# Attention's value products with queries in the partitions, head norms one tick earlier, K's decay copied ahead of the sigmoid, and three reorderings

## The reference, cut to what matters

```python
f = lb + (1.0 - lb) * sigmoid(f_pre);  log_f = log(f);  k = 1.0 - f
# per chunk: b = cumsum(log_f)
# o = (q * exp(b)) @ state + intra-chunk attention
k_dec = kc * exp(b_last - b)
new_state = exp(b_last) * state + k_dec.T @ vc
o = rms_norm(o, hgrn_norm_w) * silu(g_h)     # norm over each head's 128 columns
y = concat([pool_out, o]) @ w_out
```

```python
s = (q_nope @ k_nope.T + q_rope @ k_rope.T) * SCALE      # 8 heads, 512 queries, 768 keys
p = softmax(s);  attn = p @ v                            # v has 64 columns a head
x_mid = layer_norm(ALPHA * x + g1 * (concat([conv, attn]) @ w_o + b_o))
x = layer_norm(ALPHA * x_mid + g2 * (conv_ffn(x_mid * (1 + sc2) + sh2)))
```

## Time and profile before

| what | value |
|---|---|
| median of 3 runs | 1263.81 us (1262.99 to 1265.47) |
| profiled execution, own time | 1265.41 us |
| its span | 1263.6 us |
| TensorE matmuls busy | 1148.3 us (91%) |
| TensorE weight loads busy | 933.3 us (74%) |
| VectorE busy | 847.6 us (67%) |
| ScalarE busy | 561.5 us (44%) |
| GpSimd busy | 163.1 us (13%) |
| mean granted clock of TensorE | 0.971 |
| chain that ended last | TensorE 63%, VectorE 17%, ScalarE 12% |

### The profile page before, as it was taken

One profiled execution on the slowest core, in us unless ns is written; L12 is line 12 of the kernel. 1 busy time (PEld: TensorE's weight loads), 2 busy tenths in 40 slices (PEclk: granted clock), 3 DMA queues, 4 the chain that ended last, 5 costly groups with the idle time before them and its releaser, 6 DMA issues.

```text
span 1263.6 us, 14090 instructions
## 1 busy us (share of the span) xinstructions
PE 1148.3 (91%) x5488; PEld 933.3 (74%) x5488; DVE 847.6 (67%) x1352; ACT 561.5 (44%) x861; POOL 163.1 (13%) x179
## 2 busy tenths in 40 slices
PE   1878989898889998998999998879999999999996
PEld 1657877787778877887887765558888888888885
DVE  5866787877775775455688888838676566665246
ACT  3265445454452332657444565534644444442121
POOL 0033323441444220000000001000000000000000
PEclk9889999999999998998999999989999999999998
DMA  7723132223242567592221010011232222225201
GB/s 283 299 101 134 67 133 101 100 97 137 84 142 91 217 229 201 179 73 70 79 74 42 3 67 34 33 34 67 79 122 100 100 96 84 91 96 183 100 34 66
DMA packets 28306, 136.59 MB, mean 108 GB/s; under 512 B 7760, under 2 KB 8016, under 8 KB 14416
## 3 DMA queue, kind: packets, MB, share of 16 engines
q1 hardware_dynamic: 20448, 128.46, 29.3%
q10 hardware_dynamic: 7792, 7.24, 3.0%
HBM read 133.57 MB, written 2.12 MB: 107 GB/s over the span
## 4 chain that ended last, share of the span: by engine, by line
PE 63%; DVE 17%; ACT 12%; issue 3%; POOL 3%; DMA 2%; DVEq 0%; SPq 0%; ACTq 0%
PE PB L184 62%; ACT L199 4%; DVE RAW L1342 3%; DVE CV L213 3%; ACT WH L198 3%; DVE WL L205 2%; DMA RAW<-in_wstream 1%; DVE PTA L205 1%; DVE UPA L205 1%; POOL UPA L205 1%; DVE PX L236 1%; DMA XL<-in_xT 1%; ACT PTA L199 1%; DVE XL L213 1%; DVE AT L233 1%
## 5 line engine op out<-in xcount | busy, mean ns | idle before, releaser
L184 PE MATMUL PB<-HH,WH 128*128 128x512 f32 (+1 forms) x896 | 354.6, 396 | 18.2 <-DVE WL L205 7.4
L184 PE MATMUL PB<-HL,WH 128*128 128x512 f32 (+1 forms) x896 | 343.1, 383 | 0.0
L184 PE MATMUL PB<-HH,WL 128*128 128x512 f32 (+1 forms) x896 | 343.0, 383 | 0.0
L205 DVE TENSOR_TENSOR WL<-RAW,WH 128x1024 fp32r<-128x1024 f32 (+2 forms) x174 | 201.8, 1166 | 207.5 <-ACT WH L198 206.8
L198 ACT ACTIVATE WH<-RAW 128x1024 fp32r<-128x1024 f32 (+2 forms) x174 | 169.5, 980 | 363.7 <-PE PB L184 328.2
L184 PEld LDWEIGHTS PB<-HH,WH 128*128 128x128 f32 x896 | 172.0, 192 | 52.5 <-DVE WL L205 9.0
L184 PEld LDWEIGHTS PB<-HH,WL 128*128 128x128 f32 x896 | 171.2, 191 | 33.4
L184 PEld LDWEIGHTS PB<-HL,WH 128*128 128x128 f32 x896 | 171.8, 192 | 29.1 <-issue 0.5
L213 DVE SCALAR_TENSOR_TENSOR CV<-VP,PC,CV 128x512 f32<-128x512 f32 x120 | 89.0, 776 | 0.7
L199 ACT ACT_TABLE_LOAD x53 | 68.0, 1283 | 5.5 <-DMA PC<-in_params 4.6
L184 PE MATMUL PB<-WL,AH 128*128 128x512 f32 x176 | 68.5, 389 | 0.0
(11 more groups left out here) (266 smaller groups left out, 1840.8 us busy)
## 6 DMA issues: line engine op xcount, KB each, us to landing
RAW<-in_wstream SPq DMA_DIRECT2D x108, 1024.0 KB, 4.8
RAW<-in_wstream SPq DMA_DIRECT2D x5, 768.0 KB, 4.1
RAW<-in_wstream SPq DMA_DIRECT2D x5, 512.0 KB, 3.4
XL<-in_xT SPq DMA_DIRECT2D x2, 1024.0 KB, 8.5
HB<-in_x SPq DMA_DIRECT2D x2, 1024.0 KB, 6.2
out<-XL SPq DMA_DIRECT2D x8, 256.0 KB, 2.0
ROWS<-in_rows ACTq DMA_DIRECT2D x3, 512.0 KB, 7.6
XC<-in_ctx SPq DMA_DIRECT2D x1, 1024.0 KB, 8.2
```

The costliest lines, as they stand in the source:

```text
L184: return self.put(lambda e: e.matmul(o, l, r, start=start, stop=stop, skip_group_check=skip))
L205: return self.put(lambda e: e.tensor_tensor(o, a, b, op))
```

## The change

The diff does six things.

1. `stream_layout`: for the last pool group (g = 0) the third `also()` is left out; that "a" item and those behind it come one place later in the list.
2. HGRN: the copy into KDT becomes `key_decay` and stands at the head of `head(h, 1)` of the next head, ahead of its sigmoid and logarithm (for head 7 in `pool_gate`); DG, its spread and the product with it come three steps earlier each.
3. Before the second input product, ScalarE and VectorE split fewer blocks ahead of the first tiles of h2, tile 1 follows tile 0, and `y_squares(2, 1)` moves behind a split.
4. Attention: the exponentials become the stationary operand, 128 queries at a time, and V with one column of ones (65 columns) the moving one: four products in place of one, with queries in the partitions. VectorE's `values_out` takes a reciprocal of the sums and multiplies into OT; TensorE's `pair_turn` transposes OT of a pair into a bank of the turn (t = 3 of heads 2, 4 and 6, and at the end), from where ScalarE and VectorE split it. ScalarE's copies, logarithm and exponential and VectorE's pair product go.
5. `conv_square` of tiles that end late comes behind the last exponential.
6. Merge: the first split of the second half comes ahead of the others, and TensorE makes the first block's products of row tiles 3 and 0 of the second half ahead of the rest of the first half.

```diff
@@ -70,7 +70,8 @@
         w(u[1])
-        also()
+        if g:
+            also()
     def rows(name, *tiles):
@@ -470,7 +471,8 @@
     VG = sb("VG", [128, 6, 768], F32, c2)
-    SU = TMP[:, 0:512]
+    OTT = OT[:, :].rearrange("p (j n) -> p j n", n=128)
+    RSUM = TMP[:, 0:4].rearrange("p (j n) -> p j n", n=1)
     CKH, CKL = (z[:, 3:6, :].rearrange("p a n -> p (a n)").rearrange("p (k n) -> p k n", n=NKEY) for z in (CH, CL))
@@ -789,11 +791,6 @@
                 a.act(x, x, ACTF.Exp).then_inc(S_.a_s, ("kd", h))
-            elif step == 8:
-                a.wait_ge(S_.p_sm, ("kt", h))
-                if h:
-                    a.wait_ge(S_.p_sm, ("kv", h - 1))
-                a.copy(KDT[:, :], aux.of(("kt", h))).then_inc(S_.a_ax, ("kt", h))
             elif step == 13:
@@ -806,9 +803,17 @@
                     hgrn(h, step)
+        def key_decay(h):
+            a.wait_ge(S_.p_sm, ("kt", h))
+            if h:
+                a.wait_ge(S_.p_sm, ("kv", h - 1))
+            a.copy(KDT[:, :], aux.of(("kt", h))).then_inc(S_.a_ax, ("kt", h))
         def head(h, b):
...
             z = main.of(("z", h, b))
+            if h and b == 1:
+                key_decay(h - 1)
             a.wait_ge(S_.p_blk, 4 * h + b)
@@ -893,6 +898,8 @@
             after(nb)
+            if p == 3 and m:
+                key_decay(7)
             if p == 3:
@@ -1045,14 +1052,15 @@
         shifted(1)
-        y_squares(2, 1)
         split(B_IN2)
-        split(B_IN2 + 1)
         split(B_IN2 + 2)
         h_tile("h2", 0, 0, M2, SC1)
+        h_tile("h2", 1, 0, M2, SC1)
+        split(B_IN2 + 3)
+        y_squares(2, 1)
         y_squares(3, 1)
-        split(B_IN2 + 3)
-        for k in range(1, 8):
+        split(B_IN2 + 1)
+        for k in range(2, 8):
             h_tile("h2", k, 0, M2, SC1)
@@ -1163,26 +1171,9 @@
             a.act(PR[s % 3], main.of(("s", h, t)), ACTF.Exp, scale=SCALE).then_inc(S_.a_ev, ("s", h, t))
-        def values_out(h):
-            me, other = ((0, 64), (64, 128)) if h % 2 == 0 else ((64, 128), (0, 64))
-            z = aux.of(("ov", h))
-            a.wait_ge(S_.p_sm, ("o", h, 5))
-            if h > 1:
-                a.wait_ge(S_.v_h, ("m", 4 + h // 2 - 1))
-            a.copy(OT[me[0]:me[1], :], z[me[0]:me[1], :])
-            a.copy(SU[me[0]:me[1], :], z[other[0]:other[1], :]).then_inc(S_.a_ax, ("ov", h))
-        def pair_divisor(p):
-            a.wait_ge(S_.a_ax, ("ov", 2 * p + 1))
-            a.act(SU, SU, ACTF.Ln).then_inc(S_.a_s)
-            a.wait_ge(S_.a_s)
-            a.act(SU, SU, ACTF.Exp, scale=-1.0).then_inc(S_.a_s, ("su", p))
         def pair_high(p):
-            a.wait_ge(S_.v_s, ("pair", p))
-            a.copy(MH[:, 4 + p, :], OT[:, :]).then_inc(S_.a_h, ("m", 4 + p))
+            a.wait_ge(S_.p_sm, ("ot", p))
+            a.copy(MH[:, 4 + p, :], main.of(("ot", p))).then_inc(S_.a_h, ("m", 4 + p))
         def conv_square(j):
@@ -1215,10 +1206,6 @@
                     split(KEY_BLOCK[(h + 1) // 2] + NW)
-                if t == 1 and h:
-                    values_out(h - 1)
-                if t == 2 and h % 2 == 0 and h:
-                    pair_divisor(h // 2 - 1)
                 if 1 <= t <= 4 and h < 7:
@@ -1234,18 +1221,17 @@
                 for j in range(4):
-                    if CONV_END[j] != "end" and 6 * CONV_END[j][0] + CONV_END[j][1] + 2 == 6 * h + t:
+                    if CONV_END[j] != "end" and 6 * CONV_END[j][0] + CONV_END[j][1] + 2 == 6 * h + t < 44:
                         conv_square(j)
...
             a.dma(row, VEC[1 + n:2 + n, :].partition_broadcast(128)).then_inc(S_.row, *["o"] * n, by=16)
-        values_out(7)
         for j in range(4):
-            if CONV_END[j] == "end" or 6 * CONV_END[j][0] + CONV_END[j][1] + 2 >= 48:
+            if CONV_END[j] == "end" or 6 * CONV_END[j][0] + CONV_END[j][1] + 2 >= 44:
                 conv_square(j)
-        pair_divisor(3)
         pair_high(3)
+        split(B_O + NW)
         for j in range(4):
@@ -1264,7 +1250,7 @@
                 .then_inc(S_.a_st, (stage, "q", i, h))
-        for nb in range(B_O, B_O + 4):
+        for nb in range(B_O + 1, B_O + 4):
             split(nb + NW)
@@ -1470,11 +1456,11 @@
                     .then_inc(S_.v_ax, ("st", h))
-            elif step == 18:
+            elif step == 15:
                 v.wait_ge(S_.g_s, ("pow", h))
...
                 diag(DG, sct(h % 2)[:, 4:8], 4, ("dg", h))
-            elif step == 21:
+            elif step == 18:
                 v.wait_ge(S_.p_sm, ("dg", h))
@@ -1658,13 +1644,14 @@
         x1(1)
-        for n in range(3):
-            split(B_IN2 + n)
         gated(3, 1)
+        split(B_IN2)
+        split(B_IN2 + 2)
         h_low("h2", 0, 0)
+        h_low("h2", 1, 0)
+        split(B_IN2 + 3)
         before_power(1)
-        split(B_IN2 + 3)
-        h_low("h2", 1, 0)
+        split(B_IN2 + 1)
         before_second(1)
@@ -1797,13 +1784,24 @@
             v.maxneg(NM[:, c:c + 1], PB[2 + (j % 2 if h == 0 else 0)][:, 0:NKEY]).then_inc(S_.v_ax, ("mx", h, j), ("mx2", h, j))
-        def pair(p):
-            v.wait_ge(S_.a_s, ("su", p))
-            v.tt(OT[:, :], OT[:, :], SU, MUL).then_inc(S_.v_s, ("pair", p))
+        def values_out(h):
+            z = aux.of(("ov", h))[:, 0:260].rearrange("p (j n) -> p j n", n=65)
+            o, one = (1, 0) if h % 2 else (0, 64)
+            v.wait_ge(S_.p_sm, ("o", h, 5))
+            if h > 1:
+                v.wait_ge(S_.p_sm, ("ot", h // 2 - 1))
+            if h:
+                v.wait_ge(S_.v_ax, ("ov", h - 1))
+            v.recip(RSUM[:, :, :], z[:, :, one:one + 1]).then_inc(S_.v_s)
+            v.wait_ge(S_.v_s)
+            v.tt(OTT[:, :, 64 * (h % 2):64 * (h % 2) + 64], z[:, :, o:o + 64], RSUM[:, :, :].broadcast_to([128, 4, 64]), MUL)\
+                .then_inc(S_.v_ax, ("ov", h))
         def pair_low(p):
-            lo(ML[:, 4 + p, :], OT[:, :], MH[:, 4 + p, :], ("m", 4 + p), ("m", 4 + p))
+            v.wait_ge(S_.a_h, ("m", 4 + p))
+            v.tt(ML[:, 4 + p, :], main.of(("ot", p)), MH[:, 4 + p, :].bitcast(F32), SUB).then_inc(S_.v_ev, ("ot", p))
         query(0)
@@ -1821,6 +1819,8 @@
             for t in range(6):
+                if t == 1 and h:
+                    values_out(h - 1)
                 if 1 <= t <= 4 and h < 7:
@@ -1828,8 +1828,6 @@
                     key_low(h + 2)
-                if t == 3 and h % 2 == 0 and h:
-                    pair(h // 2 - 1)
                 if t == 3 and h < 6:
@@ -1844,8 +1842,9 @@
         conv("end")
-        pair(3)
+        values_out(7)
         pair_low(3)
+        split(B_O + NW)
         st = aux.of("cvs")
@@ -2137,7 +2136,7 @@
                 sums(bk, XR[3], 4, 0).then_inc(S_.p_sm, ("st", h))
-            elif step == 20:
+            elif step == 17:
                 spread(("dg", h), DG, 4, ("dg", h))
@@ -2188,13 +2187,16 @@
             return op
-        def by_token(bks, blocks, name, alone=False, turn=None):
+        def by_token(bks, blocks, name, alone=False, turn=None, early=()):
             for i in range(4):
...
                         turn()
-                    op = rows(bks, nb, xs, alone and n == 0, n == 3, (i,), i == 3)
+                    if n == 0 and i in early:
+                        continue
+                    op = rows(bks, nb, xs, alone and n == 0, n == 3, (i,), i == (2 if early and n == 0 else 3))
                 if i < 3:
@@ -2344,8 +2346,19 @@
             pe.wait_ge(S_.a_ev, ("s", h, t))
-            c = 192 * (h // 2) + 64 * (h % 2)
-            pe.mm(bk, VG[:, t, c:c + 128], PR[(6 * h + t) % 3], t == 0, t == 5).then_inc(S_.p_sm, ("o", h, t))
+            c = 192 * (h // 2) + 127 * (h % 2)
+            for j in range(4):
+                op = pe.mm(bk[:, 65 * j:65 * j + 65], PR[(6 * h + t) % 3][:, js(j)], VG[:, t, c:c + 65], t == 0 and j == 0, t == 5,
+                           True)
+            op.then_inc(S_.p_sm, ("o", h, t))
+        def pair_turn(p, at):
+            bk = take(("ot", p), at)
+            pe.wait_ge(S_.v_ax, ("ov", 2 * p + 1))
+            for j in range(4):
+                op = pe.tr(bk[:, js(j)], OT[:, js(j)], IDN[:, :])
+            op.then_inc(S_.p_sm, ("ot", p))
         query(0)
@@ -2370,12 +2383,16 @@
                     n += 1
+                if t == 3 and h and h % 2 == 0:
+                    pair_turn(h // 2 - 1, 2 + n % 2)
+                    n += 1
                 if (h, t) in ((1, 3), (1, 4), (2, 3)):
...
         values(7, 5)
+        pair_turn(3, 2)
         def conv_sums():
@@ -2390,9 +2407,10 @@
         def merged(k):
-            return [(MH[:, j, :], ML[:, j, :], (S_.v_h, ("m", j))) for j in (k, k + 1)]
+            return [(MH[:, j, :], ML[:, j, :], (S_.v_h, ("m", j)) if j < 4 else (S_.v_ev, ("ot", j - 4))) for j in (k, k + 1)]
         ys = [take(("oy", i, 0), i) for i in range(4)]
+        ys2 = {}
         for n, k in enumerate((4, 6, 0, 2)):
@@ -2400,9 +2418,13 @@
```

(10 more changed lines are left out.)

## The result

The changed kernel is slower: median 1279.0 us (1277.2 to 1282.1, 4 runs) against 1263.4 us (1260.0 to 1265.5, 4 runs), a ratio of 1.0129 (95% interval 1.0098 to 1.0159), some 16 us. Its profiled execution took 1278.1 us (span 1276.3, mean granted clock 0.967). The prediction said 1262.7 with a range of 1254 to 1270.

The account below looks back on a forecast made before the run. TensorE plus the gaps that others leave it was taken to set the time. Terms 1.8 (heads) - 3.4 (layout) - 3.7 (h2) + 4.2 (attention, merge) = -1.1 gave 1264.3 us, 1262.7 as a median; range 1254 to 1270.

Parts of the forecast that it names:

- Step 3: Stream layout, TensorE's wait ending at 477.45: VectorE's sum comes earlier, -3.4 us (range -4.9 to -2.5).
- The term put at 0: Stream layout: the ada dots move some ticks later, where VectorE is idle: 0, or 1 us were it not.
- Step 2: HGRN heads, diagonals DG three steps earlier: TensorE waits 3.4 for them against 2.38, +1.8 us in all.
- the rival that priced every diagonal at a whole product: HGRN heads: every diagonal waits for a whole GpSimd product, +24 in place of +1.8, total 1285 us; chance 0.03.
- +0.2 in five heads: HGRN heads with earlier diagonals: net cost of 0.2 us in each of five heads, +0.4 in two others.
- The claim on HB's wait: HGRN heads: some 0.8 us of each head is given back by the wait for HB (6.3 over eight).
- Step 1: HGRN heads, KDT's copy ahead of the sigmoid: the wait passes to Q,SS, gain 0 (bounds 0 and 9.9 us).
- Step 4: h2 reordering, TensorE's wait of 6.20 at 579: it goes on at 575.3, -3.7 us (range -5 to -2.5).
- Step 5: Attention: bank exchanges, transposes and VectorE's divisions end the taps 7.5 us later; +4.2 with the merge (range -3 to +9).
- The exchange rival: Attention: VectorE's chain has no slack up to the last tap, taps end 10.1 later, total 1267.6 us; chance 0.23.
- (f): Behind the taps, up to the merge: exponential no longer waits for them; reciprocal, product and transposes take 1.25: -1.0 us.
- (g): Merge: the 12 products moved ahead fill, with 2.8 us, TensorE's gap of 3.10 at 851.57; of that -2.3.

Follow-up runs that it names:

- experiment 2: The kernel before with the stream layout changed and the context's load (XC) issued one place earlier in SyncE's list: 0.9987, -1.6 us.
- experiment 1: The kernel before with the stream layout alone changed: 1.0036, +4.5 us.
- experiment 9: The kernel before with both HGRN edits (KDT's copy ahead, diagonals with their use three steps earlier) and nothing else: 1.0050, +6.3 us.
- experiment 8: The kernel before with only the norm diagonals, their spread and the product three steps earlier: 1.0042, +5.3 us.
- experiment 7: The kernel before with only KDT's copy moved ahead of the sigmoid: 1.0006.
- experiments 7 and 11: KDT's copy ahead of the sigmoid, in the kernel before alone (1.0006), and together with diagonals built three steps earlier but used at their old place (0.9990).
- experiment 3: The kernel before with the reordering ahead of h2 alone: 0.9973, -3.4 us.
- experiment 5: The kernel before with the attention and merge parts alone, pair transposes in the fourth aux bank instead of a main bank: 1.0022, +2.8 us.
- experiment 14: The kernel before with stream layout, context's load ahead, h2 reordering, merge's edit, and diagonals built three steps earlier with their use left: 0.9917, median 1250.4 us.
- experiment 4: The kernel before with the attention and merge parts (items 4, 5 and 6 of the change) alone: 1.0095, +12 us.

## Why the prediction was wrong

**Step 3 failed, in its last sentence:** "The ada dots move some ticks later, where VectorE is idle: 0, or 1 were it not." As far as VectorE goes the 0 was right: in experiment 2 the dots run as late, and the stretch from 477 on takes 102.2 us against 102.3. But the dots also free a slot, SyncE's next fetch waits for that slot, and the context's load stands behind this fetch in SyncE's order. It came 11 us later (8.6 later counted from the product at 477), ScalarE's chain of statistics with it, and TensorE 4.3 us later instead of 3.7 earlier. The term put at 0 measured 8.3 us in that stretch (110.5 in experiment 1 against 102.2 in experiment 2), and 8 by medians. This is the largest miss of the sum. The step's first half held for the gap, 6.54 to 3.56, but only 1.4 of its 3.4 reached the product at 477, as a wait of 1.29 for a split came ahead of it.

**Step 2's size was off.** The mechanism held in its times, 2.38 and 3.20 against 2.44 and 3.4. The Trainium skill's exclusive lock (SBUF — State Buffer, "SBUF: two separate sides") is not settled by that: with GpSimd's products at 0.79 each (4.74 / 6), four full waits and four diagonals of 0.21 would be 4.0 us, and 2.38 were measured, some 0.4 more for each diagonal. So the rival that priced every diagonal at a whole product was wrong, but these rows do not exclude shorter waits, each for the rest of a product already under way. The term that was mis-sized is "+0.2 in five heads": it took the clock as it was. With waits for SS and DG in one head the low clock took a second share in four heads of the profiled execution, at 1.5 us each. Measured: +6.2 us in the heads there, but +2.1 in the execution of experiment 9 with the same edits, and -0.2 in that of experiment 8, which has the diagonals' edit alone. The forecast of +1.8 is thus near the executions in which no more than one head has the second share. The claim on HB's wait (0.8 a head given back) was wrong by half: it spread 6.3 over eight heads, of which 4.0 lie ahead of the heads, and 0.4 a head was given back.

**Step 1 was right.** The wait passed to Q,SS at the time worked out (80.4 us behind the first Q,SS in experiment 7; 186.5 - 106.2 = 80.3 was forecast), and the copy's move gained nothing in two settings (experiments 7 and 11).

**Step 4 was right in kind**, 3.1 for 3.7 in the wait, and 3.4 by medians in experiment 3.

**Step 5 was right in place, and partly by luck in size:** +8.5 for +7.5 at the taps' end. The transposes and waits were 1.21 with a transpose of 0.44 for 1.8, 2.06 for 2.05 to 2.4, 2.16 for 1.35; the divisions 0.60; most value products 1.00 for their eight records of 128x65, for 1.05. But it held no term for the clock, up to 5 us by the estimate above, nor one for TensorE's waits for the maxima (PX), which are 4.5 us together before and 2.2 after. The two misses point in opposite directions, and no run tells them apart. Alone the part, with the merge, cost 12 us, and experiment 5 shows that 9 of them are the bank exchange and the clock behind it. The exchange rival (1267.6) was the nearest in mechanism; but it too lacked the clock and the load.

**(f) failed and (g) was too small.** (f) forecast -1.0 behind the taps and measured +0.4: the last transposes stand in a bank that the merge takes, one more bank exchange, a wait of 1.41 for which the prediction had no term. In experiment 5, with the aux bank, the merge starts 1.4 behind the last tap, 0.9 earlier than before, as (f) has it. (g) forecast -2.3 and measured -3.5, of which 1.2 is paid behind the merge, a stretch that the prediction held unchanged. The merge's edit alone gave -1.6.

What stays open: why the medians of the whole change stand 15.6 us apart and the profiled executions 12.7. The falls of the clock differ from one execution to the next (an unchanged stretch of heads took 281.6 to 283.6), and one execution of experiment 8 held a single stall of 5.29 in TensorE that none of its edits explains (last section). For the same reason the part of the HGRN edits in the 16 us is known only from medians (+6.3).

## What to carry to other kernels

When an edit moves a reader of a streamed buffer, follow the loading engine's list past the fetch that now waits: everything behind it moves too, and a load that looks unrelated may be the one that counts. Take operands' production early but leave their consumer where it was, until the trace shows it waiting; moving both turned a gain of 4 us into a loss of 5 by medians. When a new temporary needs a PSUM bank, look for one whose last user is done, not the next of a turn that others share. And hold a term for the fall of the clock behind a new wait in TensorE, as a range from 0 to the price of a fall (here 1.5 us in a head): the same waits had it in one head and not in the next.

## What the runs showed of the hardware

- The price of a fall of the clock, and that the waits alone do not fix it: in experiment 14 four heads with the same waits (DG's product 1.70 to 1.72, KDT 1.39 to 1.41) took 39.43 and 39.47 us at a mean clock of 1.00 and 41.02 and 41.04 at 0.96, 1.6 us for the fall. In experiment 4 two heads with a wait for DG of 2.39 and 2.38 took 39.78 at 1.00 and 41.07 at 0.96, 1.3 us. The head at 0.92 above took 1.5 more than the one at 0.96.
- ScalarE issues stores (vectors<-PX) from its own queue, and in one execution this held it up. In that of experiment 8, the four stores that took 2.3 us before (two rows, 1.01 and 1.24) took 14 us, ScalarE's next split came only behind them, and TensorE waited 5.29:

```profile
543.98 14.05 ACTq L180 DMA_DIRECT2D vectors<-PX  x4
558.08 1.06 ACT L198 ACTIVATE WH<-RAW 128x1024 fp32r<-128x1024 f32 x1 [13.12 <-issue]
```
